# A decoder trunk with four recurrent groups: constant products placed ahead of TensorE's waits

## The reference, cut to what matters

```python
for l in range(DEPTH):                       # DEPTH = 2, D_MODEL = 1024, D_FF = 2816
    x = x + 0.5 * rmsnorm(swiglu(rmsnorm(x, ns[0]), gate[0], up[0], down[0]), ns[1])
    mix, states = token_mixers(rmsnorm(x, ns[2]), pos, p, st, chunk)
    x = x + rmsnorm(mix, ns[3])
    x = x + 0.5 * rmsnorm(swiglu(rmsnorm(x, ns[4]), gate[1], up[1], down[1]), ns[5])

def token_mixers(h, ...):                    # four groups of 4 heads of 64
    proj = h @ w_in                          # shared input projection
    # retention, SSD, gated delta rule, mLSTM; each, chunk by chunk:
    #   att = (q k^T) * decay
    #   o   = att v + (q * inter) state
    #   state = state * carry + (k * tail)^T v
    # the gated delta rule first solves a unit triangular system per chunk and head
    return concat(out_ret, out_ssm, out_gdn, out_ml) @ w_out
```

## Time and profile before

| what | value |
|---|---|
| median of three runs | 1801.04 us |
| lowest, highest | 1800.76, 1806.31 us |
| span of the profiled execution, first to last instruction | 1796.3 us |
| its own time | not listed apart from the span; the median run is 4.7 us longer than the span |
| PE busy | 1592.9 us, 89% |
| VectorE busy | 903.6 us, 50% |
| ScalarE busy | 556.7 us, 31% |
| mean granted TensorE clock | 0.871 |
| recurrent groups of layer 0 | from about 401 to 621 us |
| recurrent groups of layer 1 | from about 1277 to 1500 us |

### The profile page before, as it was taken

How to read it: one execution, slowest core, us unless ns; L and a number is a source line. 1 busy time by engine, 2 the same in 40 slices (tenths; PEclk the granted TensorE clock), 3 DMA queues, 4 the chain that set the end, 5 groups by cost and what they waited for, 6 DMA issues and landing times.

```text
span 1796.3 us, 28795 instructions
## 1 busy us (share of the span) xinstructions
PE 1592.9 (89%) x10846; PEld 1492.3 (83%) x10846; DVE 903.6 (50%) x1415; ACT 556.7 (31%) x752; POOL 164.9 (9%) x249
## 2 busy tenths in 40 slices
PE   4999989988787789999889999899788888899995
PEld 3999979977775679999879999799687757799994
DVE  4455455645454555553455544566363544655433
ACT  3333344440011143333353333454200111533331
POOL 6000000100133320000000000001002413000000
PEclk9999999988755589999989999899695556899997
DMA  8455443430011144554334545254101102255440
GB/s 194 149 166 164 159 136 116 148 101 1 3 30 33 12 115 139 164 164 139 117 121 163 164 152 176 71 165 129 48 1 26 26 14 64 95 163 163 142 163 27
DMA packets 184921, 194.17 MB, mean 108 GB/s; under 512 B 7284, under 2 KB 181700, under 8 KB 184688
## 3 DMA queue, kind: packets, MB, share of 16 engines
q1 hardware_dynamic: 176864, 178.27, 30.7%
q0 software_dynamic: 7376, 10.91, 3.5%
q10 hardware_dynamic: 576, 3.59, 0.5%
HBM read 186.55 MB, written 6.19 MB: 107 GB/s over the span
## 4 chain that ended last, share of the span: by engine, by line
PE 84%; DVE 7%; issue 5%; ACT 2%; DMA 1%; DVEq 0%; ACTq 0%; SPq 0%; POOL 0%
PE ps L468 82%; PE ps L471 2%; DVE y L1253 1%; DVE ring_r L1212 1%; DMA ring<-in_ffn_w_up 1%; DMA big<-in_x_sample 1%; DVE y L1670 0%; DVE arena L1483 0%; DVE x L1254 0%; ACT lnr L967 0%; DVE big L1590 0%; DVE big L1709 0%; ACT rrow L968 0%; DVE y L1227 0%; DVE Sbd L1552 0%
## 5 line engine op out<-in xcount | busy, mean ns | idle before, releaser
L1212 DVE TENSOR_TENSOR ring_r<-ring,whigh_r 128x2048 fp32r<-128x2048 f32 (+1 forms) x174 | 389.9, 2242 | 466.4 <-ACT whigh_r L945 466.1
L945 ACT ACTIVATE whigh_r<-ring 128x2048 fp32r<-128x2048 f32 (+1 forms) x174 | 326.2, 1875 | 481.6 <-PE ps L468 471.8
L468 PE MATMUL ps<-hdn,whigh_r 128*128 128x288 f32 x2016 | 328.4, 305 | 24.7 <-ACT hdn L955 15.0
L468 PEld LDWEIGHTS ps<-hdn,whigh_r 128*128 128x128 f32 x2016 | 292.3, 192 | 37.1 <-issue 31.8
L468 PE MATMUL ps<-hdn,ring_r 128*128 128x288 f32 x2016 | 315.9, 300 | 0.0
L468 PE MATMUL ps<-y_r,whigh_r 128*128 128x288 f32 x1888 | 293.4, 299 | 0.0
L468 PEld LDWEIGHTS ps<-hdn,ring_r 128*128 128x128 f32 x2016 | 288.1, 193 | 0.0
L468 PEld LDWEIGHTS ps<-y_r,whigh_r 128*128 128x128 f32 x1888 | 268.8, 191 | 0.0
L468 PE MATMUL ps<-big_r,whigh_r 128*128 128x288 f32 x832 | 130.4, 298 | 7.5 <-DVE arena_r L1212 7.5
L468 PEld LDWEIGHTS ps<-big_r,whigh_r 128*128 128x128 f32 x832 | 117.4, 190 | 8.5 <-issue 8.3
L468 PE MATMUL ps<-big_r,ring_r 128*128 128x288 f32 x704 | 110.9, 299 | 0.0
(11 more groups left out here) (328 smaller groups left out, 1624.4 us busy)
## 6 DMA issues: line engine op xcount, KB each, us to landing
ring<-in_ffn_w_gate SPq DMA_DIRECT2D x44, 1024.0 KB, 5.2
ring<-in_ffn_w_up SPq DMA_DIRECT2D x44, 1024.0 KB, 5.2
ring<-in_ffn_w_down SPq DMA_DIRECT2D x32, 1024.0 KB, 5.1
ring<-in_w_in SPq DMA_DIRECT2D x30, 1024.0 KB, 5.0
ring<-in_ffn_w_down SPq DMA_DIRECT2D x16, 768.0 KB, 4.4
ring<-in_w_out SPq DMA_DIRECT2D x8, 1024.0 KB, 5.4
cst<-in_const ACTq DMA_DIRECT2D x1, 2301.0 KB, 8.3
big<-in_x_prompt ACTq DMA_DIRECT2D x1, 1024.0 KB, 11.4
```

Source lines behind the costliest of these rows:

```text
L468: return pe.matmul(out, lhsT, rhs, start=start, stop=stop, **k)
L945: A(whighR[:, pos % 2, 0:rows * 256], ring[:, s, 0:rows * 256], ACT.Copy)\
L1212: return TT(out, in_, high, ALU.subtract)
```

## The change

Inside PE's `mixer` a helper, `turning(n)`, issues n products of the constant matrix `rot` with the constant matrix of ones, 128x128x128 in float32, into the last quarter of PSUM bank 4 (`gdn`) or 6 (the others). Nobody reads that place. Calls of it stand ahead of the waits, behind two of them, and ahead of each round of the sample state additions. `ssd` gets one further wait, on `snat_read`.

```diff
+                def turning(n):
+                    for _ in range(n):
+                        mm(ps[:, 4 if m == "gdn" else 6, 384:512], C("rot"), ones)
+
                 hold(sem("mixed_ready"), l * 4 + mi + FREE)
+                if m in ("ret", "ml"):
+                    turning(6)
...
                 if m == "gdn":
                     gdn_solve(l, l1)
+                if m == "ssd":
+                    hold(sem("snat_read"), l * 4 + 4)
+                turning(2)
                 hold(sem("qbd_ready"), l * 4 + mi + 1)
...
                             g.then_inc(sem("ks_done"), 1)
+                        turning(2)
                         hold(sem("resid_ready"), l * 3 + c + 1)
...
+                    turning(2)
                     hold(sem("probs_ready"), l * 12 + 3 * mi + c + 1)
                     hold(sem("values_ready"), l * 12 + 3 * mi + c + 1)
+                    turning(1)
                     if c or mi:
                         hold(sem("raw_ready"), l * 12 + 3 * mi + c)
...
                         scores(2)
+                    turning(2)
                     hold(sem("vw_ready"), l * 12 + 3 * mi + c + 1)
...
+                        turning(4)
                         hold(sem("kx_ready"), l * 4 + mi + 1)
                         hold(sem("state_read"), l * 8 + 2 * mi + 2)
                         for n in range(4):
+                            turning(1)
                             if n >= 2:
                                 hold(sem("sadd_read"), l * 16 + 4 * mi + n - 1)
```

## The result

The changed kernel takes 1819.62 us (median of 4 runs, 1808.57 to 1825.09) beside 1801.43 us for the kernel before on the same chip (4 runs, 1800.76 to 1806.31): 1.0082 times as long, interval 1.0054 to 1.0109. It is slower by 0.8%, by the medians by 1.0%; the forecast was 1794 us, and the time lies 7 us above the range.

What follows compares the result with a forecast made beforehand. PE, largely at half clock in the recurrent groups, was taken to bound the kernel. Price 73.0 plus wait 1.2, less 147.6 f at f = 0.55, gave -7 us from 1801.04: 1794 us, range 1775 to 1813.

Steps and rivals of the forecast that it cites:

- PE and its clock bound these stretches: Solver's end to output projection, eight stretches: PE busy about 80% at clock 0.50 to 0.62; at most 111.2 us come back.
- A: Rival: the clock holds nearly everywhere in the groups, f 0.75 or more; -37 us, 1764 us; chance 12%.
- C: Rival: the added products do nothing to the clock, f = 0; +74 us, 1875 us; chance 4%.
- Mean clock of the stretches about 0.75: Granted clock of the eight stretches, solver's end to output projection, was to rise from 0.56 to about 0.75.
- f = 0.55: Share of half-clock work in the eight stretches turning to full clock; 74.2 - 147.6 f gives -7 us.
- The price: 164 of 236 products on PE's path: 36.6 us at full clock (0.223 each), 73.0 at half (0.445 each).
- Hidden: 36 of 118 in a layer: Products in PE's waits: 24 at hand-overs to chunks 1 and 2, 8 in `gdn`, 4 at chunk 0; they cost nothing.
- rival B: Each group's tail, at the state additions, takes back more than the chunks win; +15 us, 1816 us at f = 0.40; 29%.
- `gdn` faster by several us, `ssd` least or up: Time between two group ends: down by several us in `gdn`, down least or up in `ssd`.
- The added wait, 1.2 us: In `ssd`, the wait on VectorE's copy of the turned states costs 0.6 us, twice: 1.2 us.
- The six at the start only cost: Start of `ret` and `ml`: transposes alone raise the clock; if the six were needed they would win some 6 us.

Runs made afterwards that it cites:

- e1_narrow: The change with its 236 constant products using only 4 of 128 rows: 1902.94 us, 1.0543 of the kernel before.
- e3_no_rounds: The change without the single product ahead of each round of state additions (204 products stay): 1792.26 us, 0.9897 of the kernel before.
- e6_only_covered: The change with only 48 products kept, ahead of waits in which PE idled before: 1791.82 us, 0.9914 of the kernel before.
- e7_moved: The change with 200 products, none in the rounds, moved ahead of waits such as `mixed_ready` and `state_read`: 1755.56 us, 0.9694 of the kernel before.
- e10_moved_narrow: e7_moved with its 200 products using 4 of 128 rows: 1847.86 us, 1.0234 of the kernel before.
- e9_together: The change with the four products of the rounds put together ahead of `kx_ready` (still 236): 1794.37 us, 0.995 of the kernel before.
- e8_change_again: The change unedited, run again on another chip: median 1822.4 us of 10 runs, 1794.17 to 1837.97, 1.0037 of the kernel before.
- e5_wait_only: The change without any constant products, only the reordered wait in `ssd` left: 1808.74 us, 1.0012 of the kernel before.
- e4_no_start: The change without the six products at the start of `ret` and `ml` (212 stay): 1817.15 us, 1.0026 of the kernel before.
- e12_other_values: The change with dense cosine and sine tables as operands instead of the sparse matrix and ones: 1831.24 us, 1.0131 of the kernel before.

## Why the prediction was wrong

The accounts that decide, in the manner of the one above (own profiled runs; n is the number of new products):

```
us, eight stretches   total |  n  | new products (at half) | other PE work (at half) | PE idle
e1_narrow             401.8 | 236 | 117.4 (106.6)          |  251.2 (231.7)          | 33.4
e3_no_rounds          296.9 | 204 |  73.9 (34.6)           |  184.2 (92.0)           | 38.5
e6_only_covered       297.7 |  48 |  20.9 (12.9)           |  229.7 (184.7)          | 46.9
e7_moved              266.9 | 200 |  67.2 (28.6)           |  175.0 (66.6)           | 24.6
e10_moved_narrow      355.7 | 200 |  92.4 (81.5)           |  251.1 (233.8)          | 12.1
e9_together           299.8 | 236 |  82.1 (36.6)           |  178.8 (79.6)           | 38.9
e8_change_again       346.7 | 236 | 100.9 (69.7)           |  208.6 (142.4)          | 36.9
```

- *PE and its clock bound these stretches, and products of 128 rows raise it.* Right. `e1_narrow` against the change shows it: as many products with 4 rows raise nothing, with 128 they do. Rivals A and C fell.
- *Mean clock of the stretches about 0.75.* Right for the profiled run: 0.73.
- *f = 0.55.* By the account f is 1 - 107.1/228.9 = 0.53 in the profiled run, 57.2 us back for the 61.2 foreseen. By groups it is 0.67 for `gdn` (0.65 foreseen), 0.62 for `ret` (0.60), 0.56 for `ml` (0.55) and 0.32 for `ssd` (0.45). But it is 0.38 in the run at 1838 us. So the second step that failed, the smaller one, is to give f as one number: the same kernel has 0.53 in one run and 0.38 in another, and the range ended at 0.42. The median of the runs (1819.6) lies 12.6 us above the profiled span, and the forecast carried the 4.7 us of before over. Of the miss of 26 us, some 8 lie here.
- *The price: 164 products exposed, at the two rates of the earlier trace rows.* This is the step that failed first, the term that was mis-sized most. At f = 0.55 the 236 products should have taken 76 us of PE (0.32 each); they took 90.9 (0.385). The rate was read between products of the same shape, and these come in small blocks among other shapes. In twos and threes one takes 0.31 at full and 0.53 at half clock, alone in the rounds 0.42 and 0.73. The twos and threes make up about 11 us of what the products took over the two rates, the single ones about 5, the large blocks under 2; somewhat more of them ran at full clock than f = 0.55 has it, so 15 of these 18 us are left. What a single one does to the rounds beside it (0.56 in all at full clock) comes on top and is in the other work.
- *Hidden: 36 of 118 in a layer.* 72 of them at 0.32 are 23 us; 22.8 of PE's idle time went. Right in size, but not in place: at `state_read` and at the solver's end the prediction named the gap and did not see that a wait stands ahead of the products (1.18 us in `ret`, 1.5 at the solver's end). `e7_moved` puts them ahead of `state_read`, and its idle time is 24.6 us.
- *The tail (rival B).* The right place and the right sign: no net gain in the tail of `ret` even at full clock (7.14 for 7.01 us). B stood at 29% and 1816 us. It was to decide from f below 0.50, with the tails at half clock. In fact the kernel was slower at 0.53, and 19 of the 24 single products ran at full clock; in `ret` each cost 2.5 times the rate put on it. That the place decides is shown by `e9_together` and `e3_no_rounds`, 25 and 27 us below the change; by which way, the price or the clock behind it, only in part.
- *`gdn` faster by several us, `ssd` least or up.* Half right: `gdn` 32.8 in one layer and 40.2 in the other, `ssd` 53.1 (43.6 before) and 40.7.
- *The added wait, 1.2 us.* Right within what can be measured (`e5_wait_only`).
- *The six at the start only cost.* The reading behind it does not hold. In layer 1 of before the same transposes left `ret` at half clock for 10.7 us, and so did `e4_no_start` in both layers (9.3 and 9.9 us); with the six it is 3.0 to 5.8. Layer 0 of before was the exception among eight cases, and one row could not carry the reading. Whether the six earn their price is not settled.

In a sum for the profiled run: foreseen 53 for the price net of cover, 1.2, -61.2: -7. Measured 90.9 - 22.8 - 57.2: +11. Of the 18 us between, 14 are the price and 4 the clock.

## What to carry to other kernels

Filler that keeps TensorE's clock up pays here by its place: ahead of a wait (and ahead of every wait that stands in front of that one) it hides as far as the wait is long, in one block ahead of small products it costs its own time, in twos and threes a fifth to two fifths more (0.53 for 0.445, 0.31 for 0.223), singly among small products about twice that. So measure its price apart from its effect, with the same instructions made too narrow to act, and look at several runs and both layers, since the clock makes a kernel's time spread. When the engine already arrives at full clock, a few products in the waits keep it (`gdn`, 9 us of 39 for 12 products), which is where to begin.

## What the runs showed of the hardware

- A matrix product's rows matter for the granted clock, not only its being there: 4 of 128 rows left the groups of layer 0 at 0.53 to 0.59, 128 rows gave 0.73 to 0.88 in layer 0 of the change and 0.53 to 0.95 in layer 1. Denser values changed nothing that could be seen (`e12_other_values`).
- A 128-row product alone between products of 32 rows costs more than its rate among its own kind: 0.42 us for 0.223 at full clock, and four 32-row products beside it take 1.03 us instead of 0.93, which makes 0.56.
- With unchanged instructions one group took quite different times (`ssd`: 40.7 or 53.1 us), and the two layers of one run may differ.
- Without filler at its start `ret` stood at half clock for 9.3 to 11.1 us in seven of eight cases, with six products there for 3.0 to 5.8 us in all twelve.
